# The expert weights w1 and w3 in four transfers: halves of the contraction, each with a wait of its own

## The reference, cut to what matters

```python
D_MODEL = 1024
N_EXPERTS = N_GROUPS * EXPERTS_PER_GROUP
D_EXPERT = D_MODEL // 2
...
    def expert_block(args):
        xb, e = args
        hid = jax.nn.silu(xb @ w1[e]) * (xb @ w3[e])
        return hid @ w2[e]
```

## Time and profile before

| | us |
|---|---|
| three runs | 1583.48, 1585.27, 1585.30 |
| profiled execution, first to last instruction (span) | 1584.0 |
| PE busy | 1476.6 |
| DVE busy | 980.7 |
| 192 transfers of expert weights, 2048 KB each | 26.9 from issue to landing (median) |

### The profile page before, as it was taken

One profiled execution on the slowest core, in us unless ns is written; L12 is line 12 of the kernel. 1 busy time (PEld: TensorE's weight loads), 2 busy tenths in 40 slices (PEclk: granted clock), 3 DMA queues, 4 the chain that ended last, 5 costly groups with the idle time before them and its releaser, 6 DMA issues.

```text
span 1584.0 us, 45784 instructions
## 1 busy us (share of the span) xinstructions
PE 1476.6 (93%) x18897; PEld 1002.0 (63%) x18898; DVE 980.7 (62%) x2114; ACT 474.0 (30%) x798; POOL 25.8 (2%) x64
## 2 busy tenths in 40 slices
PE   8999999999989989988999999989899897997978
PEld 6788888765555556545778875458655554554545
DVE  5346642377767767765744357852777675675755
ACT  6442221412222222221543355533222221221211
POOL 3000000000000000000000000000000000000000
PEclk9999999999999999998999999999999998999989
DMA  6331332989999999999431322125899999999996
GB/s 220 119 106 54 107 106 69 389 331 429 429 428 427 430 428 427 429 430 428 179 106 55 121 80 81 40 74 245 357 389 427 429 429 429 427 429 429 428 428 277
DMA packets 55482, 461.12 MB, mean 291 GB/s; under 512 B 4496, under 2 KB 4640, under 8 KB 30848
## 3 DMA queue, kind: packets, MB, share of 16 engines
q1 hardware_dynamic: 51728, 453.00, 69.0%
q10 hardware_dynamic: 2192, 4.23, 0.8%
q0 software_dynamic: 1504, 3.07, 0.7%
HBM read 458.15 MB, written 2.13 MB: 291 GB/s over the span
## 4 chain that ended last, share of the span: by engine, by line
PE 72%; DMA 22%; DVE 4%; issue 2%; SPq 0%; ACT 0%; DVEq 0%; ACTq 0%
DMA EB<-in_m_w 22%; PE ps L1479 15%; PE ps L1317 10%; PE ps L1319 10%; PE ps L1318 10%; PE ps L1468 7%; PE ps L1490 6%; PE ps L1450 4%; PE ps L1705 2%; PE ps L1740 1%; PE ps L1759 1%; PE ps L1774 1%; PE ps L1592 1%; PE ps L1313 1%; PE ps L1379 1%
## 5 line engine op out<-in xcount | busy, mean ns | idle before, releaser
L1479 PE MATMUL ps<-EB,SCR 128*32 128x256 f32 x6016 | 364.4, 397 | 72.5 <-DMA EB<-in_m_w 59.7
L1479 PEld LDWEIGHTS ps<-EB,SCR 128*32 128x32 f32 x6016 | 195.7, 114 | 233.4 <-issue 105.1
L995 DVE TENSOR_TENSOR X<-X,ps 128x1024 f32 x188 | 221.1, 1218 | 28.9 <-PE ps L1450 28.9
L1319 PE MATMUL ps<-EB_r 128*128 128x512 f32 x512 | 200.2, 391 | 0.0
L1468 PE MATMUL ps<-H,SCR 128*32 128x256 f32 x3072 | 185.6, 382 | 0.0
L1490 PE MATMUL ps<-EB,SCR 128*32 128x256 f32 x3008 | 179.5, 379 | 0.0
L666 ACT ACTIVATE SCR_r<-ps,SCR 128x256 f32 x94 | 44.5, 474 | 443.4 <-PE ps L1490 443.4
L986 DVE TENSOR_TENSOR SCR<-SCR,ps 128x128 f32<-128x128 f32 x94 | 37.0, 393 | 211.6 <-ACT SCR L663 211.6
L1490 PEld LDWEIGHTS ps<-EB,SCR 128*32 128x32 f32 x3008 | 97.7, 110 | 64.5 <-DVE SCR L989 0.4
L1318 PE MATMUL ps<-EB_r 128*128 128x512 f32 x352 | 137.5, 391 | 0.0
L1468 PEld LDWEIGHTS ps<-H,SCR 128*32 128x32 f32 x3072 | 90.4, 110 | 62.1
(11 more groups left out here) (280 smaller groups left out, 1667.0 us busy)
## 6 DMA issues: line engine op xcount, KB each, us to landing
EB<-in_m_w SPq DMA_DIRECT2D x192, 2048.0 KB, 26.9
EB<-in_a_w_in SPq DMA_DIRECT2D x7, 2048.0 KB, 8.2
EB<-in_a_w_out SPq DMA_DIRECT2D x4, 2048.0 KB, 7.9
EB<-in_kv_w SPq DMA_DIRECT2D x4, 2048.0 KB, 12.6
EB<-in_b_w_qg SPq DMA_DIRECT2D x4, 2048.0 KB, 7.9
EB<-in_b_w_out SPq DMA_DIRECT2D x2, 2048.0 KB, 9.4
X<-in_x SPq DMA_DIRECT2D x4, 512.0 KB, 6.9
EB<-in_a_w_in SPq DMA_DIRECT2D x4, 512.0 KB, 9.7
```

The lines of the kernel that those rows point to most:

```text
L995: add = v.tensor_tensor(X_t, X_t, moved[1][:, :, t, :], ALU.add)
L1319: return mm(o, left[1], right[0], start=False, stop=stop)
L1479: last = mm(ps[0][g * CAP:(g + 1) * CAP, 0:2 * P].rearrange("p (w n) -> p w n", w=2), xT[:, k, :], w13_sb[s][:, :, k, g * P:(g + 1) * P], ...
```

## The change

Each of w1 and w3 comes as two transfers, one for the steps k = 0 to 3 of the contraction and one for k = 4 to 7. The first halves of both count up `w13_half0`, the second halves `w13_half1`. PE waits for the first pair ahead of k = 0 and for the second ahead of k = 4; behind k = 3 it counts up a new semaphore, `up_half`. For a later expert SP waits for `up_half`, issues the two first halves, waits for `up`, issues the two second halves, and goes on to w2 as before. The load semaphores are now shared by the two layers, with the count of the second layer's loads raised by that of the first's.

```diff
--- before.py
+++ after.py
...
-                "logits", "tables", "sel", "up", "silu", "hid", "gath", "xg", "hidT",
+                "logits", "tables", "sel", "up_half", "up", "silu", "hid", "gath", "xg", "hidT",
...
-            moe[l]["w13"] = sems(f"moe{l}_w13_", NBUF)
-            moe[l]["w2"] = sems(f"moe{l}_w2_", NBUF)
+        w13_loaded = [sems(f"w13_half{q}_", NBUF) for q in range(2)]
+        w2_loaded = sems("w2_loaded", NBUF)
...
+        HK = KD // 2
...
                     w, to = (m_w1, w1_sb) if part == 1 else (m_w3, w3_sb)
-                    sp.dma_start(to[s], w[l, e].rearrange("(p k) n -> p k n", k=KD)).then_inc(m["w13"][s], 16)
+                    for q in range(2):
+                        ks = slice(q * HK, (q + 1) * HK)
+                        sp.dma_start(to[s][:, ks, :], w[l, e].rearrange("(p k) n -> p k n", k=KD)[:, ks, :])\
+                            .then_inc(w13_loaded[q][s], 16)
...
-                sp.wait_ge(m["up"], ended)
...
-                sp.dma_start(w1_sb[s], w1e).then_inc(m["w13"][s], 16)
-                sp.dma_start(w3_sb[s], w3e).then_inc(m["w13"][s], 16)
+                for q, product in enumerate(("up_half", "up")):
+                    ks = slice(q * HK, (q + 1) * HK)
+                    sp.wait_ge(m[product], ended)
+                    sp.dma_start(w1_sb[s][:, ks, :], w1e[:, ks, :]).then_inc(w13_loaded[q][s], 16)
+                    sp.dma_start(w3_sb[s][:, ks, :], w3e[:, ks, :]).then_inc(w13_loaded[q][s], 16)
                 sp.wait_ge(m["down"], ended)
...
                 def expert(s, loads, r0, r1, gather_last=False):
+                    loads = loads + l * first_loads(s)
                     with pe.Fori(r0, r1) as n:
 
-                        pe.wait_ge(m["w13"][s], 32 * loads)
+                        pe.wait_ge(w13_loaded[0][s], 32 * loads)
                         pe.wait_ge(m["xT"], n + 1)
                         for k in range(KD):
+                            if k == HK:
+                                last.then_inc(m["up_half"], 1)
+                                pe.wait_ge(w13_loaded[1][s], 32 * loads)
                             for g in range(CG):
...
```

More of the change, by code:

```diff
@@ L375, in slot, with first_loads @@
             return (e + 1) % NBUF
+        def first_loads(s):
+            return len([e for e in range(NE) if slot(e) == s])
+        HK = KD // 2
         block = ctx.enter_context(nc.Block())
@@ L394, in load_expert @@
             def load_expert(l, e, parts=(1, 3, 2)):
-                m, s = moe[l], slot(e)
+                s = slot(e)
                 for part in parts:
                     if part == 2:
-                        sp.dma_start(w2_sb[s], m_w2[l, e].rearrange("(p c) n -> p c n", c=KE)).then_inc(m["w2"][s], 16)
+                        sp.dma_start(w2_sb[s], m_w2[l, e].rearrange("(p c) n -> p c n", c=KE)).then_inc(w2_loaded[s], 16)
                         continue
                     w, to = (m_w1, w1_sb) if part == 1 else (m_w3, w3_sb)
-                    sp.dma_start(to[s], w[l, e].rearrange("(p k) n -> p k n", k=KD)).then_inc(m["w13"][s], 16)
+                    for q in range(2):
+                        ks = slice(q * HK, (q + 1) * HK)
+                        sp.dma_start(to[s][:, ks, :], w[l, e].rearrange("(p k) n -> p k n", k=KD)[:, ks, :])\
+                            .then_inc(w13_loaded[q][s], 16)
             def load_later_expert(l, e, s):
@@ L411, in load_later_expert @@
                 w2e = m_w2[l][bass.ds(expert, 1), :, :].rearrange("a (p c) n -> p (a c) n", c=KE)
-                sp.dma_start(w1_sb[s], w1e).then_inc(m["w13"][s], 16)
-                sp.dma_start(w3_sb[s], w3e).then_inc(m["w13"][s], 16)
+                for q, product in enumerate(("up_half", "up")):
[3 more added lines that the diff above has]
+                    sp.dma_start(w3_sb[s][:, ks, :], w3e[:, ks, :]).then_inc(w13_loaded[q][s], 16)
                 sp.wait_ge(m["down"], ended)
-                sp.dma_start(w2_sb[s], w2e).then_inc(m["w2"][s], 16)
+                sp.dma_start(w2_sb[s], w2e).then_inc(w2_loaded[s], 16)
             def moe_loads(l):
@@ L1485, in expert @@
                         pe.wait_ge(m["hidT"], n + 1)
-                        pe.wait_ge(m["w2"][s], 16 * loads)
+                        pe.wait_ge(w2_loaded[s], 16 * loads)
                         for c in range(KE):
```

## The result

The changed kernel takes 1589.78 us (median of 8 runs, 1587.37 to 1591.09), the kernel before 1584.97 us (8 runs, 1583.48 to 1585.48). The ratio is 1.003, with the 95% interval 1.0021 to 1.0039: slower by 4.8 us. I had forecast +0.6 us, 1585.9 us, with a range of 1582.2 to 1589.8 us. The median lies inside the range by 0.02 us, at its upper end, and that is luck: my own sum for the slower rival ended at 1589 us, and I had given no term for what the range has above that. The mechanism that I had called the slower rival, small pieces that cost more than the quiet rows say, is what happened.

The account below looks back on a forecast made before the run. The prediction took the transfers to bound the two mixtures. Per layer, 2.3 us for smaller pieces less 1.6 us for the earlier start gave +0.7 us; twice that less 0.84 gave +0.6 us, 1585.9 us, range 1582.2 to 1589.8 us.

Parts of the forecast that it names:

- slower rival: In the full queue of 28 experts, small pieces cost 8.1 ns or more; at 9.0 ns 1589 us; chance 10%.
- The mixtures are bound by the transfers: In both mixtures of experts, 64 experts' weights take 941 us, PE's 94 items 780 us, so the transfers decide.
- first rival: In both mixtures PE's 18 waits for weights are each cut by 1.83 us, giving about 1543 us; chance 3%.
- Term 1: At each mixture's head, the earlier release restarts the idle queue sooner: 1.6 us gained a layer, ends 0.8 and 1.83.
- second gap: The later of two idle stretches of the transfer queue at each mixture's head; said to end 1.6 us earlier.
- Term 2: In each mixture's full queue, each extra piece costs 5.2 ns: 2.3 us a layer, ends 0 and 4.0.
- the row of 404 GB/s: Rate of 2 KB projection tiles in a quiet stretch; gave the price of 5.2 ns for each extra piece.
- sum 2D - 0.84: Whole span: D for each of two layers, less 0.84 us at layer 0's end: +0.6 us, ends -4.4 and +5.6.
- D: Shift of each layer's last weight landing, Term 2 less Term 1: +0.7 us, ends -1.8 and +3.2.
- Layer 0 shifts by D - 0.84: At layer 0's last down product, where PE had been late: its start shifts by -0.1 us.
- fourth rival: At layer 1's end PE's clock falls behind new waits, adding 2.6 us: 1588.5 us; chance 4%.
- A fixed time for each transfer: In the mixtures' queue each of 112 extra transfers costs time; at 0.1 us each, 11 us, 1597 us; chance 2%.

Follow-up runs that it names:

- e3: Kernel before, with halves and early release only for the fourth and fifth expert of each layer, all others whole: 1582.41 us, ratio 0.9980.
- e9: Kernel before, with halves and early release for the fourth expert of each layer alone: 1585.15 us, ratio 0.9999.
- e1: Kernel before, with w1 and w3 still in whole transfers but read in 8 KB pieces: 1593.12 us, ratio 1.0052.
- e5: Kernel before, with each w1 and w3 transfer split into even and odd rows, pieces still 16 KB: 1585.36 us, ratio 1.0002.
- e7: Kernel before, with w1 and w3 in whole transfers read in 2 KB pieces: 1644.34 us, ratio 1.0377.
- e6: Kernel before, with w1 and w3 in four transfers each, 4 KB pieces, old waits: 1610.22 us, ratio 1.0162.
- e10: Changed kernel, with 14 unused small matmuls on PE ahead of each layer's last wait for w2: 1588.23 us, ratio 1.0020.
- e4: Changed kernel, with SP issuing an expert only when w1 and w3 of the one before have landed: 1592.74 us, ratio 1.0052.

## Where the prediction was right and where it was wrong, step by step

- **"The mixtures are bound by the transfers"**: right. The share is 1.01 again, and the waits for weights kept their sum, 59.0 us for 59.7. I had expected about half of it at the up product; the other half came back there as waits for the second halves. Where both halves are awaited, as in the rows at 561.62 and 566.51 us, what PE gains at the first half it waits away at the second. The first rival (1543 us) is out. (The nines of layer 1 begin at slice 29, not 30 as I wrote; nothing rests on it.)
- **Term 1, -1.6 us a layer**: right. The second gap ends 1.6 and 1.7 us sooner; in e3 the last landings have this gain without the rest. That the first gap adds nothing is shown by e9.
- **Term 2, the step that failed.** I priced an extra piece at 5.2 ns and a layer at 2.3 us; measured are 9.6 ns and 4.25 us. The rate was to be 425 to 426 GB/s and is 424 and 423. The mechanism was right (e1: pieces alone; e5: transfers free) and the size was off. I took the row of 404 GB/s as "a queue that nothing else disturbs", and set the row of 388 aside because other queues were at work. The same shape in the mixtures' full queue moves 381 to 389 GB/s (e7). So the row that I set aside was the nearer one, and its 9.0 ns would have made a forecast of 1589 us, for 1589.8 measured. It is this mis-sized term that puts the time 3.9 us above the forecast and at the very end of the range. What lowers the price in the stretch of 404 no run here shows.
- **The sum 2D - 0.84**: right as a form where PE stands at its last down product before w2 lands. With D = 2.6 it gives +4.4 us, the difference of the two spans, and it gives the times of e1, e6 and e7 within 2 us. It doesn't hold where PE is late, as in layer 1 of e3, or of e1, where the down product starts 0.96 us behind the landing; that e1 comes out so close is in part luck.
- **Layer 0 shifts by D - 0.84**: right in size (1.84 us for 2.6 - 0.84 = 1.8), but two things that I hadn't seen cancel in it. PE, now ahead, no longer waits 1.59 us for DVE in front of the moves, and the down product takes 1.6 us longer at the fallen clock. I had this clock fall as the fourth rival and had put it at layer 1's end, where the product kept its 1.93 us behind a wait of 1.87 us. Against the trace of e10 the low clock costs 1.6 us at the moves of layer 0, of which 0.8 us are left at the first product of layer 1.
- **A fixed time for each transfer** (the fifth rival): out by e5.
- **SP's held issues** I hadn't foreseen; e4 shows that they cost no rate.

Of "slower by over 0.2%" I had said 14%, and this was too little: two rows stood at 5.2 and 9.0 ns, either side of the 8.1 ns that decides, and nothing on the page made the lower one much the likelier.

## What to carry to other kernels

Where the queue of transfers is full, a split costs by its pieces and not by its transfers: count the extra pieces on each engine, and take their price from the rows where the queue is full with other work around it. Split only the transfers ahead of which the queue stands empty, here 2 of the 29 experts of a layer that come behind a release, or, where the consumer doesn't need halves of the contraction, split by partitions so that the pieces keep their length (here such a split would release nothing earlier, as every step of the contraction reads all 128 partitions). A shorter wait on an engine that isn't the bound gives nothing; where it starts the transfers earlier, only the last gap ahead of the full stretch counted here.

## What the runs showed of the hardware

- An extra piece in a full queue cost an engine 9.2 to 9.6 ns, the same for pieces of 8, 4 and 2 KB beside those of 16 KB. The Trainium skill's page "DMA: Bandwidth & Descriptors", section "Measured (HBM→SBUF, 128 partitions, SWDGE, issued from GpSimd)", has about 10.5 ns for each packet of a 4 KB transfer issued from GpSimd. The runs have a price of like size, paid on top of the bytes' time even at 8 KB; whether it is the same cost no run here shows.
- The additional 128 transfers and their 2,048 small packets cost nothing that can be measured (e5: 1.0002).
- With 8 KB pieces SP was held up to 8.65 us (after, 320 transfers) and 9.71 us (e1, 192 transfers) in the issue of one transfer, while the share of the transfers stayed at 1.01; with 16 KB pieces the longest weight issue in the mixtures took 0.59 us (before, 192 transfers) and 0.69 us (e5, 320 transfers). What limit it meets is open.
- In after, a wait of 1.97 us ahead of one product was followed by the low clock (3.53 us for 1.93), and one of 1.87 us ahead of another wasn't, though PE had waited another 1.59 us some 3 us before it. In e4 one of 3.06 us was (3.64 us), and one of 1.95 us wasn't (1.93 us). In the trace with fourteen small matmuls in the wait of layer 0 the product took 1.93 us.
